# Gate products of a recurrent layer in three passes of split operands, with a new order of its three engines

## The reference

```python
xy = rmsnorm(x, a_norm) @ w_in + b_in          # 1024 -> 2048
xb, yb = split(xy)                             # recurrent branch, gate branch
gate = gelu(yb)
xc = causal_conv4(xb) + conv_b                 # per channel
r = sigmoid(xc_block @ gate_w[0] + gate_b[0])  # 8 blocks of 128 channels
i = sigmoid(xc_block @ gate_w[1] + gate_b[1])
log_a = -8 * r * softplus(-lam);  a = exp(log_a)
bx = sqrt(-expm1(2 * log_a)) * (i * xc)
hs[t] = a[t] * hs[t-1] + bx[t]
x = x + (hs * gate) @ w_out
```

## Time and profile before

| | |
|---|---|
| median of 3 runs | 1038.23 us (1037.96 to 1038.48) |
| profiled execution | 1039.88 us, span of its core 1038.1 us |
| TensorE matmul busy | 1021.4 us, 98% of the span |
| VectorE busy | 821.0 us, 79% |
| ScalarE busy | 652.8 us, 63% |
| recurrent stage, input tiles | 6.48 to 110.56 us |

### The profile page before, as it was taken

One profiled execution on the slowest core, in us unless ns is written; L12 is line 12 of the kernel. 1 busy time (PEld: TensorE's weight loads), 2 busy tenths in 40 slices (PEclk: granted clock), 3 DMA queues, 4 the chain that ended last, 5 costly groups with the idle time before them and its releaser, 6 DMA issues.

```text
span 1038.1 us, 15457 instructions
## 1 busy us (share of the span) xinstructions
PE 1021.4 (98%) x5984; PEld 887.6 (86%) x5984; DVE 821.0 (79%) x1173; ACT 652.8 (63%) x956; POOL 143.9 (14%) x197
## 2 busy tenths in 40 slices
PE   8999999999999999999999999999999999999995
PEld 6777889989989989988888888889979979979984
DVE  7988886896896895898657777676797797697696
ACT  7698776655755755755436767776764664654655
POOL 1000211131121121100000000211022022022022
PEclk9999999999999999999999999999999999999999
DMA  7222866598498498472311212846399599588672
GB/s 269 82 83 68 223 145 184 119 250 231 117 245 239 117 248 234 124 179 82 123 62 60 65 59 61 224 112 156 119 207 233 169 202 232 175 188 229 191 173 91
DMA packets 47592, 165.29 MB, mean 159 GB/s; under 512 B 5408, under 2 KB 5536, under 8 KB 47392
## 3 DMA queue, kind: packets, MB, share of 16 engines
q0 software_dynamic: 24768, 87.04, 37.6%
q1 hardware_dynamic: 22320, 76.03, 21.7%
q10 hardware_dynamic: 432, 1.24, 0.3%
HBM read 159.05 MB, written 2.10 MB: 155 GB/s over the span
## 4 chain that ended last, share of the span: by engine, by line
PE 82%; DVE 7%; DMA 4%; issue 4%; ACT 2%; POOL 0%; SPq 0%; DVEq 0%; ACTq 0%; POOLq 0%
PE ps L2043 27%; PE ps L1910 23%; PE ps L2078 21%; PE ps L2141 4%; DVE w_lo L1161 3%; DMA w_raw<-weights 2%; PE ps L2205 2%; PE ps L2230 2%; DMA q<-weights 2%; PE ps L1969 1%; ACT w_hi L624 1%; PE ps L2219 1%; DVE value L1540 1%; DVE r L1502 1%; DVE work L1511 0%
## 5 line engine op out<-in xcount | busy, mean ns | idle before, releaser
L2043 PE MATMUL ps<-x_hi,w_hi 128*128 128x256 f32 x896 | 254.0, 284 | 0.0
L2043 PE MATMUL ps<-x_hi,w_lo 128*128 128x256 f32 x896 | 253.7, 283 | 0.0
L2043 PE MATMUL ps<-x_lo,w_hi 128*128 128x256 f32 x896 | 253.7, 283 | 0.0
L624 ACT ACTIVATE w_hi<-w_raw 128x1024 fp32r<-128x1024 f32 x134 | 140.2, 1052 | 143.1 <-DMA w_raw<-weights 115.2
L1161 DVE TENSOR_TENSOR w_lo<-w_raw,w_hi 128x1024 fp32r<-128x1024 f32 x134 | 164.0, 1224 | 73.6 <-ACT w_hi L624 73.2
L1161 DVE TENSOR_TENSOR w_lo<-q,w_hi 128x1024 fp32r<-128x1024 f32 x144 | 176.6, 1229 | 50.6 <-ACT w_hi L624 50.0
L624 ACT ACTIVATE w_hi<-q 128x1024 fp32r<-128x1024 f32 x144 | 151.0, 1052 | 97.5 <-PE ps L2043 47.1
L2078 PE MATMUL ps<-w_hi,a_hi 128*128 128x512 f32 x448 | 176.3, 393 | 3.0 <-DVE w_lo L1161 1.8
L2078 PE MATMUL ps<-w_hi,a_lo 128*128 128x512 f32 x448 | 174.7, 390 | 0.0
L2078 PE MATMUL ps<-w_lo,a_hi 128*128 128x512 f32 x448 | 174.6, 390 | 0.0
L2043 PEld LDWEIGHTS ps<-x_lo,w_hi 128*128 128x128 f32 x896 | 172.0, 192 | 0.3
(11 more groups left out here) (227 smaller groups left out, 1709.6 us busy)
## 6 DMA issues: line engine op xcount, KB each, us to landing
q<-weights POOLq DMA_DIRECT2D x160, 512.0 KB, 6.6
w_raw<-weights SPq DMA_DIRECT2D x134, 512.0 KB, 4.3
x<-x_t SPq DMA_DIRECT2D x8, 256.0 KB, 5.5
y_t<-value SPq DMA_DIRECT2D x8, 256.0 KB, 2.3
acc<-work POOLq DMA_DIRECT2D x6, 256.0 KB, 3.5
rstd<-work POOLq DMA_DIRECT2D x6, 256.0 KB, 3.3
w_raw<-weights SPq DMA_DIRECT2D x4, 256.0 KB, 4.3
gw<-gate_weights ACTq DMA_DIRECT2D x1, 1024.0 KB, 5.1
```

The source lines that it names most:

```text
L624: nc.scalar.activation(w_hi[:, t % RING, :], src, ACT.Copy).then_inc(whi_done, 1)
L2043: ins = nc.tensor.matmul(to, w[:, t % RING, ws], o[:, op, j, :], start=fresh and j == 0 and f % 2 == 0 and n == 0, stop=j == PAIRS - 1 and ...
```

## The change

The gate weights and the convolution's result are split as the other operands are. ScalarE copies `gw` into `gw_hi` in two operations of 1024 columns, placed ahead of `split_hi(4)`, and each `lru_v[m]` into `xc_hi` (`conv_hi`, 8 of 512 columns). VectorE subtracts to get `gw_lo` (two of 1024 columns, ahead of `split_lo(4)`, `decay` and the norm) and `xc_lo` (`conv_lo`, 8 of 512). `gates(m)` now has six fp32r matmuls in place of two float32 ones, and waits for `conv_lo(m)` in place of `conv(m)`. It stands after tiles 5 (0, 1), 6 (2, 3), 8, 9, 10 and 12 in place of 4 (0), 5 (1, 2), 6, 7, 9, 10 and 12. `split_lo(5)` moves ahead of the norm's Newton step. The rest of both orders is rewritten; ScalarE's has 14 table loads in the stage. `gw_lo` lies in the place of `gw`, and `xc_hi` and `xc_lo` in that of `work`; no wait of another engine is added for that.

```diff
+            def gate_weights_hi(n):
+                ks = slice(n * TILE, (n + 1) * TILE)
+                act.wait_ge(gw_in, 16)
+                nc.scalar.activation(gw_hi[:, ks], gw[:, ks], ACT.Copy).then_inc(gw_hi_done, 1)
+
+            def conv_hi(m):
+                act.wait_ge(conv_done, m + 1)
+                if m >= 2:
+                    act.wait_ge(gates_mm, m - 1)
+                nc.scalar.activation(xc_hi[:, m % 2, :], lru_v[:, m, :], ACT.Copy).then_inc(xc_hi_done, 1)
...
             act.wait_ge(consts_done, 1)
+            gate_weights_hi(0)
+            gate_weights_hi(1)
             split_hi(4)
             split_hi(5)
             norm_guess(N_A)
+            split_hi(6)
...
+            def gate_weights_lo(n):
+                ks = slice(n * TILE, (n + 1) * TILE)
+                dve.wait_ge(gw_hi_done, n + 1)
+                nc.vector.tensor_tensor(gw_lo[:, ks], gw[:, ks], gw_hi[:, ks], ALU.subtract).then_inc(gw_lo_done, 1)
+
+            def conv_lo(m):
+                dve.wait_ge(xc_hi_done, m + 1)
+                nc.vector.tensor_tensor(xc_lo[:, m % 2, :], lru_v[:, m, :], xc_hi[:, m % 2, :],
+                                        ALU.subtract).then_inc(xc_lo_done, 1)
...
+            gate_weights_lo(0)
+            gate_weights_lo(1)
             split_lo(4)
             decay()
+            split_lo(5)
             norm_newton(N_A)
             dve.wait_ge(conv_consts, 1)
-            split_lo(5)
             branch(0)
             split_lo(6)
...
             def gates(m):
-                pe.wait_ge(conv_done, m + 1)
+                pe.wait_ge(xc_lo_done, m + 1)
                 if m == 0:
-                    pe.wait_ge(gw_in, 16)
+                    pe.wait_ge(gw_lo_done, 2)
...
-                    ins = nc.tensor.matmul(ps[:, bank, :], gw[:, ws], lru_v[:, m, :], start=True, stop=True)
+                    for i, (w, o) in enumerate(((gw_hi, xc_hi), (gw_hi, xc_lo), (gw_lo, xc_hi))):
+                        ins = nc.tensor.matmul(ps[:, bank, :], w[:, ws], o[:, m % 2, :], start=i == 0, stop=i == 2)
                 ins.then_inc(gates_mm, 1)
...
-            gates_after = {4: (0,), 5: (1, 2), 6: (3,), 7: (4,), 9: (5,), 10: (6,), 12: (7,)}
+            gates_after = {5: (0, 1), 6: (2, 3), 8: (4,), 9: (5,), 10: (6,), 12: (7,)}
```

More of the change, by code:

```diff
@@ L262, in build @@
         prob_t = sb("prob_t", [P, 2, S], F32)
+        early = ExitStack()
+        xc_hi = sb("xc_hi", [P, 2, S], F32R, early)
+        xc_lo = sb("xc_lo", [P, 2, S], F32R, early)
+        early.close()
         work = sb("work", [P, 4, S], F32)
@@ L781, in _ @@
             tap(6)
+            sigmoids(4)
+            decay_exp(3)
+            split_hi(13)
+            conv_hi(6)
+            sigmoids(5)
+            split_hi(14)
             tanh(4)
-            decay_exp(3)
+            tap(7)
+            sigmoids(6)
+            tanh(5)
             decay_exp(4)
[L785 to L790, removed]
             decay_exp(5)
             root(3)
+            conv_hi(7)
             root(4)
@@ L798, in _ @@
             gelu_of(2)
+            gated_hi(0)
             sigmoids(7)
             split_hi(16)
+            gated_hi(1)
             tanh(6)
-            split_hi(17)
             tanh(7)
             decay_exp(6)
-            gated_hi(0)
+            split_hi(17)
             decay_exp(7)
@@ L1351, in _ @@
             conv(0)
-            branch(3)
             conv(1)
             split_lo(7)
+            branch(3)
+            conv_lo(0)
             branch(4)
-            gated_input(0)
+            conv_lo(1)
+            split_lo(8)
             conv(2)
             conv(3)
+            gated_input(0)
+            conv_lo(2)
+            y_scaled(0)
             gated_input(1)
-            split_lo(8)
-            y_scaled(0)
+            conv_lo(3)
+            conv(4)
+            split_lo(9)
             gated_input(2)
-            conv(4)
+            conv_lo(4)
+            split_lo(10)
             branch(5)
-            split_lo(9)
+            gated_input(3)
             decayed(0)
-            split_lo(10)
-            gated_input(3)
             decayed(1)
+            conv(5)
             decayed(2)
             y_scaled(1)
-            conv(5)
-            scaled_input(0)
-            recurrence(0)
             split_lo(11)
             branch(6)
-            scaled_input(1)
-            recurrence(1)
-            gated_input(4)
+            scaled_input(2)
+            scaled_input(0)
+            conv_lo(5)
+            recurrence(0)
             split_lo(12)
@@ L1382, in _ @@
             y_scaled(2)
-            scaled_input(2)
+            gated_input(4)
+            split_lo(13)
+            conv_lo(6)
             decayed(3)
+            scaled_input(1)
+            branch(7)
+            recurrence(1)
             gated_input(5)
-            branch(7)
+            split_lo(14)
+            conv(7)
+            gated_input(6)
             decayed(4)
-            split_lo(13)
+            decayed(5)
             recurrence(2)
[L1390 to L1393, removed]
             y_scaled(3)
-            scaled_input(4)
-            scaled_input(5)
+            conv_lo(7)
             scaled_input(3)
             y_scaled(4)
+            recurrence(3)
             gated(0)
+            scaled_input(4)
             split_lo(15)
-            recurrence(3)
+            gated(1)
+            scaled_input(5)
+            gated_lo(0)
             recurrence(4)
             gated_input(7)
-            gated(1)
             y_scaled(5)
+            gated_lo(1)
+            recurrence(5)
             split_lo(16)
+            gated(2)
+            decayed(6)
             split_lo(17)
-            recurrence(5)
-            decayed(6)
-            gated_lo(0)
             y_scaled(6)
-            gated(2)
             gated(3)
             gated(4)
+            gated(5)
             split_lo(18)
-            gated_lo(1)
             decayed(7)
             gated_lo(2)
-            gated(5)
+            y_scaled(7)
+            gated_lo(3)
             scaled_input(6)
-            gated_lo(3)
+            gated_lo(4)
             recurrence(6)
-            y_scaled(7)
-            gated_lo(4)
             scaled_input(7)
+            gated_lo(5)
             gated(6)
-            gated_lo(5)
             recurrence(7)
```

45 lines of the change are left out of this document (28 added, 17 removed).

## The result

Over 20 runs of each, the changed kernel takes 1040.84 us (median) and the kernel before 1038.72; the ratio is 1.0019, with an interval of 1.0012 to 1.0026, so some 2.0 us are lost (1.2 to 2.7), where 0.8 us less was forecast. One of the 20 executions of the changed kernel took 1438.44 us at a mean granted clock of 0.654, and the ratio and all means leave it out. One profiled execution of each has nearly the same span, 1038.2 against 1038.1, and a single pair of traces would thus have hidden the loss. The profiled execution of the kernel before was one of its longer ones: 91 other executions of it, run beside the experiments, have a mean span of 1037.4, with 1036.0 to 1039.4 as the ends. The changed kernel's spans have a mean of 1038.9 (19 executions) and 1039.1 (11 on another chip).

A forecast was written before the change was run, and what follows sets the result against it. TensorE was taken as the bound, its matmuls filling 98% of the span. +2.26 us late start, -3.1 gates and +0.1 waits, rounded to -0.8 against the 1038.23 median, gave 1037.4 us; 8-in-10 range 1036.1 to 1039.6.

The forecast's parts named there:

- The gate products: TensorE's eight gates: six fp32r passes in place of two float32 products save 3.1 us, 2.9 at the other end.
- The splits of the gate weights: Two subtractions at the head of VectorE's queue delay tile 4 by 2.26 us, to 33.4, none hidden; ScalarE pays nothing.
- The walk through the fuller queues: Stepping through VectorE's and ScalarE's new orders in the stage: all TensorE's needs met, two narrowly; 0.1 us added for waits.
- The first rival: VectorE's waits in the changed stage exceed 4.3 us and it becomes the bound, up to 1043.2 us; chance 0.12.
- I take that the rest shifts as one piece: Behind the changed stage TensorE is again the bound, and everything later was assumed to move together.
- some tenths: Allowance for how far a shift against the DMA traffic behind the stage may move the end.
- the -0.85 of the sum: TensorE's total up to the output product: +2.26 us late start minus 3.1 saved on gates, product near 109.7.
- The clock: Rival: granted clock falls during TensorE's 2.7 us rest before tile 4, half of 4.3 us lost, 1039.5 us; chance 0.04.
- the prediction's own sign of being wrong: Forecast wrong if tile 4 starts before 32.5, TensorE waits over 1 us for xc_lo or out_lo, or clock drops.
- the reading of the earlier trace: After TensorE's last matmul the clock held through 4.3 us of rest, so a 2.7 us rest before tile 4 seemed safe.
- Its own range: The forecast case's span of times for the whole kernel, given as 1036.6 to 1038.3 us; the case had chance 0.75.
- the span plus 0.1: How the median of the runs, 1038.23 us, was related to the profiled span of 1038.1 us.

The follow-up runs named there:

- after_f32: Changed kernel with float32 gate products of lru_v and gw put back, all splits still made but not used by TensorE: 1.0030 of the kernel before.
- split_late: Changed kernel with VectorE's two subtractions for gw_lo moved from the head of its queue to behind branch(2): 1.0010 of the kernel before.
- code_shift: Changed kernel plus ten matmuls of only 8 columns behind tile 3, results unused: 0.9999 of the kernel before.
- busy_short: Changed kernel plus two float32 matmuls of 512 columns behind tile 3, 1.7 us of work: 0.9991 of the kernel before.
- after_again: Changed kernel unaltered, run beside the kernel before on another chip: 1.0019 of the kernel before.
- after_look2: Changed kernel unaltered, one profiled execution: first gates start at 46.88 us, clock at 0.50 from 34.1 to 37.5.
- after_look3: Changed kernel unaltered, one more profiled execution: first gates start at 44.87 us, clock whole at tile 4.
- keep_busy: Changed kernel plus ten full 128x512 matmuls behind tile 3, results unused, filling TensorE's rest before tile 4: 0.9994 of the kernel before.
- before_head: Kernel before with the four gate-weight operations at the head of ScalarE's and VectorE's queues, results unused, gates still float32: 1.0032 of the kernel before.
- before_shift: Kernel before plus ten matmuls of 8 columns behind tile 3, nothing else: 1.0018 of the kernel before.
- split_on_pool: Changed kernel with the two subtractions for gw_lo moved from VectorE to GpSimd: 1.0033 of the kernel before.

## Why the prediction was wrong, point by point

- **The gate products** were right: 3.1 us to save was the estimate, and `after_f32` against the changed kernel gives 2.9 in the stage.
- **The splits of the gate weights** were right: 2.26 us in full, tile 4 at 33.40 for 33.4. That the place was already a wait of TensorE's was the right thing to look at.
- **The walk through the fuller queues** was right: the first gates at 44.36 for 44.4, `conv_lo(7)` ready at 91.9 against a need of 92.0 (91.3 was forecast, and TensorE lost 0.03 us to it), the output product at 109.84 for 109.7. The first rival, VectorE as the bound, fell for this order; `split_late` shows that it comes true when TensorE is some 2 us earlier.
- **The step that failed** is "I take that the rest shifts as one piece". It was this term of the sum that was mis-sized: nothing but "some tenths" was set down for it, and between the -0.85 of the sum and the +1.5 of the mean spans stand 2.3 us, a part of which is the clock's (next point). TensorE's program is longer (16 records more), and the blocks in which it is loaded met two or three critical weight loads of the second dense layer in each of its four traces, with a gap of TensorE of 1.3 to 1.9 us behind each. `code_shift` takes these meetings away and adds a microsecond of work in a rest, and the mean span falls from 1039.1 to 1037.1.
- **The clock** was a rival with a chance of 0.04. It happened in two of four traces of the changed kernel, at 1.4 and 1.65 us, and the prediction's own sign of being wrong, a clock below 1.00 between 33 and 40, came up with it. The step that failed here is the reading of the earlier trace rows. The clock's fall 4.3 us behind the last matmul was one sample of a delay that differs from execution to execution, and was taken for a lower end: in the 17 kept traces it is 2.2 us (`busy_short`) to 5.2 us (`code_shift`). That the kernel before never rested there for over 1.2 us said only that nothing was known of 2.8.
- **The account does not close.** -0.85 as forecast, +2.0 for the program loads (the changed kernel against `code_shift`) and 0 to +1 for the clock is +1.15 to +2.15 us, which takes in the +1.5 of the mean spans. But the 2.0 is measured against `code_shift`, and not against the kernel before, where it would have to hold. By stages, in the kept traces (us; the second column runs from the first dense layer to the last wait ahead of the second, the third from there to TensorE's last matmul; 9.8 us follow in each):

| trace | start of the first dense layer | to the second | to the last matmul |
|---|---|---|---|
| before | 154.07 | 527.36 | 346.87 |
| after, after_again | 153.36, 155.07 | 527.92, 527.38 | 347.08, 346.93 |
| after_look2, after_look3 | 155.84, 153.84 | 527.41, 528.41 | 347.06, 347.16 |
| code_shift, busy_short | 153.51, 153.47 | 527.87, 528.58 | 345.24, 345.29 |
| keep_busy | 153.95 | 527.94 | 346.28 |
| before_head, after_f32 | 156.79, 156.68 | 527.82, 527.62 | 344.72, 344.22 |

The last column shows that the five versions without such meetings are 0.7 to 2.9 us shorter there than the changed kernel. It also shows that the one trace of the kernel before, 0.7 us above its mean, is only 0.1 to 0.3 shorter, though it has no meeting. So how the +1.5 us against the kernel before divides among program loads, the clock and the stretch between the dense layers (up to 1 us in these traces) stays open.
- What lies outside the span is 0.1 to 0.2 us longer in the changed kernel; why was not tried.
- `keep_busy` (0.9994) and `busy_short` (0.9991) stand where the forecast put the change (0.9992). That is in part luck: the kernel before keeps its own program loads, and `before_shift` shows that their place is worth up to 0.9 us beside the direct cost.
- Two slips of the prediction did not decide. Its own range, from the terms that it names, is 1036.8 to 1038.7 and not 1036.6 to 1038.3. And the median is not the span plus 0.1: within one execution the time is 1.8 us over the span, and the median of 1038.23 goes with a span of some 1036.4.

Open: which DMA engine a program load takes, and why one that comes as in `after_f32` (153.49, with the weight load ending at 154.10 on fifteen engines and at 154.12 on the last) does no harm. The table of the loads shows the meeting, and `code_shift` that it goes away with the program's length; the rule for when a meeting costs was not found.

## What to carry to other kernels

Before a rest of the bounding engine is made longer, ask what the clock does in it, and look at more than one execution: an event that comes in every second one is missing from half of the single traces. Where a kernel's later stages have weight loads without slack, any edit that adds or removes instructions on TensorE moves its program loads against them; so try the same edit with a few harmless instructions more before it is judged, since that alone took 2.0 us off one kernel here and put 1.7 us, 0.85 of it direct, on another. And work should go where an engine waits in any case: an accumulating load and two copies in ScalarE's wait took the subtraction off VectorE, at the price of one late weight tile that had to be moved, while the same subtraction on idle GpSimd cost VectorE 4.2 us.

## What the runs showed of the hardware

- A rest of TensorE of 2.3 to 3.0 us between two matmuls was followed by 3.4 us at 1.2 GHz in two of four traces of one program, and a rest of 2.9 us in `split_on_pool`'s; with 1.7 or 2.3 us of work in it, in neither trace, and the mean clock was 0.9972 in place of 0.9963. Behind the last matmul of a program the clock stayed whole for 2.2 to 5.2 us (17 traces).
- A load of 16 KB of program took 0.9 to 1.0 us at the places of the table, and a 512 KB load is done only when the last of its 16 engines is: 0.5 to 1.1 us later, in the cases where the two met and it was held.
- GpSimd's subtraction of 128x1024 float32, 2.8 us for each, made VectorE's operations beside it up to 2.8 times as long (3.39 for 1.22 us).
